# Hybrid decoder step on one core: the samples' latent scores from three matmuls, high and low queries side by side

## What is computed

```python
def _mla_sample(q_nope, q_rope, ckv, kr, cache_ckv, cache_kr, page_table, w_uk, w_uv):
    past_c = cache_ckv[page_table].reshape(DB, -1, MLA_KV_RANK)      # 2048 positions x 128
    past_r = cache_kr[page_table].reshape(DB, -1, MLA_ROPE)          # 2048 positions x 32
    c_all = jnp.concatenate([past_c, ckv], axis=1)
    r_all = jnp.concatenate([past_r, kr], axis=1)
    q_lat = jnp.einsum("bthd,chd->bthc", q_nope, w_uk.reshape(MLA_KV_RANK, H, MLA_NOPE))
    s = (jnp.einsum("bthc,bsc->bhts", q_lat, c_all)
         + jnp.einsum("bthr,bsr->bhts", q_rope, r_all)).astype(jnp.float32) * MLA_SCALE
    mask = jnp.arange(P + T)[None, :] <= (P + jnp.arange(T))[:, None]
    p = jax.nn.softmax(jnp.where(mask, s, NEG), axis=-1)
    o_lat = jnp.einsum("bhts,bsc->bthc", p.astype(c_all.dtype), c_all)
```

## Time and profile before

| | us |
|---|---|
| three runs | 1795.09, 1804.6, 1806.44 |
| median | 1804.6 |
| span of the profiled execution | 1796.1 |
| TensorE busy | 1722.8 (96%) |
| TensorE weight loads busy | 1506.7 (84%) |
| VectorE busy | 858.5 (48%) |
| ScalarE busy | 661.3 (37%) |
| GpSimd busy | 578.2 (32%) |

### The profile page before, as it was taken

One profiled execution on the slowest core, in us unless ns is written; L12 is line 12 of the kernel. 1 busy time (PEld: TensorE's weight loads), 2 busy tenths in 40 slices (PEclk: granted clock), 3 DMA queues, 4 the chain that ended last, 5 costly groups with the idle time before them and its releaser, 6 DMA issues.

```text
span 1796.1 us, 27967 instructions
## 1 busy us (share of the span) xinstructions
PE 1722.8 (96%) x9949; PEld 1506.7 (84%) x9949; DVE 858.5 (48%) x1800; ACT 661.3 (37%) x1326; POOL 578.2 (32%) x535
## 2 busy tenths in 40 slices
PE   7999989999997999999999999999999999999996
PEld 6788878888886888888788989888898898888985
DVE  6433336667675776766443332433423333334235
ACT  5222125667675666565422312212112121121113
POOL 1000004566561877668301312212113122121221
PEclk9999987999999999999999999999999999999999
DMA  8232243323207565655612668486595775956812
GB/s 281 103 105 94 95 124 104 93 58 101 77 7 180 166 187 154 168 159 166 219 47 52 136 137 141 124 166 112 116 156 128 154 122 125 166 110 134 150 46 104
DMA packets 156061, 227.44 MB, mean 127 GB/s; under 512 B 31063, under 2 KB 128984, under 8 KB 149528
## 3 DMA queue, kind: packets, MB, share of 16 engines
q1 hardware_dynamic: 153086, 159.39, 30.0%
q0 software_dynamic: 2880, 66.85, 22.4%
HBM read 201.12 MB, written 91.93 MB: 163 GB/s over the span
## 4 chain that ended last, share of the span: by engine, by line
PE 48%; DMA 2%; ACT 1%; DVE 1%; POOL 0%; issue 0%; SPq 0%; ACTq 0%; DVEq 0%; POOLq 0%
PE wide L2582 22%; PE turn L2604 14%; PE rest L2583 7%; PE wide L2266 4%; DMA out_y_prompt<-f_gc 1%; PE wide L2681 1%; DMA o_work<-scratch_s_o 0%; DMA acc<-in_w_gate 0%; PE turn L2278 0%; DVE f_gc L2560 0%; ACT f_gc L2497 0%; PE rest L2589 0%; POOL f_gl L2660 0%; ACT f_rows L2504 0%; POOL f_st L2428 0%
## 5 line engine op out<-in xcount | busy, mean ns | idle before, releaser
L2604 PE MATMUL turn<-lead,f_ah 128*128 128x512 f32 x792 | 245.6, 391 | 4.7 <-DVE f_al L2548 4.0
L2517 DVE TENSOR_TENSOR acc<-turn,acc 128x512 f32<-128x512 f32 x198 | 136.6, 691 | 197.5 <-PE turn L2604 197.5
L2582 PE MATMUL wide<-hT_h,lead 128*128 128x512 f32 x704 | 184.9, 354 | 0.0
L2604 PEld LDWEIGHTS turn<-lead,f_ah 128*128 128x128 f32 x792 | 148.2, 189 | 36.5 <-DVE f_al L2548 4.2
L2385 POOL TENSOR_TENSOR f_gl<-f_graw,f_gh 128x1024 fp32r<-128x1024 f32 x21 | 50.6, 2408 | 351.6 <-ACT f_gh L2435 351.6
L1054 POOL TENSOR_SCALAR a_pr<-a_pr,a_rden 128x256 f32<-128x256 f32 (+7 forms) x128 | 94.3, 747 | 191.6 <-DVE a_rden L1154 187.0
L2604 PE MATMUL turn<-lead,f_al 128*128 128x512 f32 x396 | 154.8, 391 | 0.0
L2531 DVE SCALAR_TENSOR_TENSOR f_gc<-wide,f_coef,f_gc 128x832 f32<-128x832 f32 x44 | 47.7, 1085 | 209.6 <-ACT f_lasts L2455 206.7
L761 PE MATMUL zp<-win_h,xT_h 128*128 128x512 f32 (+1 forms) x288 | 113.0, 392 | 3.3 <-DVE acc L632 3.3
L761 PE MATMUL zp<-win_l,xT_h 128*128 128x512 f32 (+1 forms) x288 | 111.7, 388 | 0.0
L761 PE MATMUL zp<-win_h,xT_l 128*128 128x512 f32 (+1 forms) x288 | 111.7, 388 | 0.0
(11 more groups left out here) (362 smaller groups left out, 4437.3 us busy)
## 6 DMA issues: line engine op xcount, KB each, us to landing
out_s_win_k<-in_state_win_k POOLq DMA_DIRECT2D x10, 3264.0 KB, 41.8
out_s_win_v<-in_state_win_v POOLq DMA_DIRECT2D x10, 3264.0 KB, 44.4
acc<-in_state_win_k SPq DMA_DIRECT2D x16, 768.0 KB, 6.1
acc<-in_state_win_v SPq DMA_DIRECT2D x16, 768.0 KB, 5.6
f_uraw<-in_w_up SPq DMA_DIRECT2D x22, 512.0 KB, 4.4
f_draw<-in_w_down SPq DMA_DIRECT2D x11, 1024.0 KB, 33.0
f_graw<-in_w_gate SPq DMA_DIRECT2D x21, 512.0 KB, 7.9
acc<-in_cache_kv_latent SPq DMA_DIRECT2D x128, 64.0 KB, 1.8
```

The lines of the kernel that those rows point to most:

```text
L2517: nc.vector.tensor_tensor(a, dp[h][:], a, ALU.add).then_inc(S["d_add"], 1)
L2582: nc.tensor.matmul(out[:, c0:c1], w[n][:, k, :], x[:, k, c0:c1], start=s, stop=e)
L2604: last = nc.tensor.matmul(dp[h][:], a[:, c, t * P:(t + 1) * P], w[:, c, h * 512:(h + 1) * 512], start=(c == 0 and j == 0), stop=(c == 1 an ...
```

## The change

The queries' high and low parts now lie in one tile m_qhl, in the order high of sample 0, low of sample 0, high of sample 1, and so on, with a strip of 64 zero columns at the end, which GpSimd clears at the block's start (semaphore q_pad; ScalarE waits for it ahead of the cast m_qr). 128 neighbouring columns are then the high and the low queries of one sample. With them as weights, a product with the high keys gives rows 0 to 63 of the bank the high queries' part and rows 64 to 127 the low queries'. A product with the low keys follows with the same weights, and the rotary product with 64 weight columns goes to rows 0 to 63: three matmuls of 512 columns. `bank_use` of event s becomes "hd": ScalarE copies rows 64 to 127 into half of the tile a_own (this tile is used by the second attention block alone before), and VectorE's instruction adds that copy where it added zeros. The copy adds a low-queries-by-low-keys term that was not there before. Event s_new keeps four matmuls, with the rotary one at another place, and its result lies in rows 0 to 63.

```diff
-        self.q_h, self.q_l = sb("m_qh", [P, DEC_B, NS], F32R), sb("m_ql", [P, DEC_B, NS], F32R)
+        self.q_hl = sb("m_qhl", [P, 2 * DEC_B + 1, NS], F32R)
+        self.q_h, self.q_l = (self.q_hl[:, 0:2 * DEC_B, :].rearrange("p (b x) n -> p b x n", x=2)[:, :, x, :] for x in range(2))
         self.q_r = sb("m_qr", [3 * ROPE, DEC_B, NS], F32R)
+        self.s_low = [prompt.own[i * NS:(i + 1) * NS] for i in range(2)]
...
-        if e[0] in ("s", "s_new"):
+        if e[0] == "s_new":
             return "d"
-        if e[0] in ("pre_uk", "pre_qn", "pre_new", "pre_lat", "cT", "fold", "p", "p_new"):
+        if e[0] in ("pre_uk", "pre_qn", "pre_new", "pre_lat", "cT", "s", "fold", "p", "p_new"):
             return "hd"
...
     def gpsimd(self, pool, e):
         S, nc = self.S, self.nc
+        if e[0] == "setup":
+            nc.gpsimd.memset(self.q_hl[:, 2 * DEC_B, :].bitcast(F32), 0.0).then_inc(S["q_pad"], 1)
...
         elif k == "pre_qr":
+            act.wait_ge(S["q_pad"], 1)
...
+        elif k == "s":
+            g = e[1]
+            if g >= 2:
+                self.ring.done(act, ("s", g - 2))
+            nc.scalar.copy(self.s_low[g % 2], bank[NS:P]).then_inc(R["bank_hi"], 1)
...
         elif k in ("s", "s_new"):
             b, h = divmod(e[1], 4) if k == "s" else (e[1], 4)
             rows = self.half(b)
-            bank = self.ring.ready(dve, e)
             if k == "s":
-                src, tab, cols = bank[rows, :], self.zero[rows, 0:512], slice(512 * h, 512 * h + 512)
+                bank = self.ring.hi(dve, e)
+                src, tab, cols = bank[0:NS, :], self.s_low[e[1] % 2], slice(512 * h, 512 * h + 512)
             else:
-                src, tab, cols = bank[rows, 0:DEC_T], self.fresh[rows, :], slice(PAST, PAST + DEC_T)
+                bank = self.ring.ready(dve, e)
+                src, tab, cols = bank[0:NS, 0:DEC_T], self.fresh[0:NS, :], slice(PAST, PAST + DEC_T)
             if e == ("s_new", 0):
                 dve.wait_ge(S["const"], 64)
-                dve.wait_ge(self.zero_in, 16)
...
-                last = nc.tensor.matmul(out, a, b, start=(i == 0), stop=(i == len(terms) - 1))
+                last = nc.tensor.matmul(out[0:a.shape[1]], a, b, start=(i == 0), stop=(i == len(terms) - 1))
...
-            pair = slice(b - b % 2, b - b % 2 + 2)
-            flat = lambda t: t[:, pair, :].rearrange("p a n -> p (a n)")
-            qh, ql, qr = flat(self.q_h), flat(self.q_l), flat(self.q_r)
+            flat = lambda n: self.q_hl[:, n:n + 2, :].rearrange("p a n -> p (a n)")
+            qh, ql, qr = flat(2 * b), flat(2 * b + 1), self.q_r[:, b, :]
...
-                product(out, ((qh, x), (qh, xl), (ql, x), (qr, y))).then_inc(R["bank_ps"], 1)
+                product(out, ((qh, x), (qr, y), (qh, xl))).then_inc(R["bank_ps"], 1)
...
-                product(out, ((qh, x), (qh, xl), (ql, x), (qr, y))).then_inc(R["bank_ps"], 1)
+                product(out, ((qh, x), (qr, y), (qh, xl), (ql, x))).then_inc(R["bank_ps"], 1)
```

More of the change, by code:

```diff
@@ L1272, in __init__ @@
             "const q_in w_in new_in c_new0 c_new1 c_new2 qn_ok q3_h q3_l w_h w_l rw3_h rw3_l pre_h "
-            "r3_h r3_l c_hi cs neg_go turn_go exp recip stored").split()}
+            "r3_h r3_l c_hi cs neg_go turn_go exp recip stored q_pad").split()}
         for i in range(3):
@@ L1475, in mine @@
     def mine(self, t, i):
-        return t[:].rearrange("p b (i e t) -> p e b i t", i=PAIRS, e=2)[:, i]
+        return t.rearrange("p b (i e t) -> p e b i t", i=PAIRS, e=2)[:, i]
     def latent(self, bank):
```

## The result

| | median us | lowest to highest | ratio to before, 95% interval |
|---|---|---|---|
| before, 20 runs beside it | 1799.22 | 1793.18 to 1806.44 | |
| after, 20 runs (the range leaves out one of 3382.04) | 1806.69 | 1800.58 to 1809.75 | 1.0038 (1.0028 to 1.0049) |

What follows compares the result with a forecast made beforehand. TensorE, busy in 96% of the span, was taken to set the pace. Removed matmuls of -7.4 us plus 2.5 us of added waits gave -4.9 us, from the median 1804.6 to 1799.7, forecast as 1800; range 1788 to 1810.

Steps and rivals of the forecast that it cites:

- the likeliest case: Whole kernel: 3 to 7 us below the median, given 45%; the forecast itself was a gain of 4.9 us.
- 32 x 0.23 = 7.4 us removed: TensorE, first attention block: one of four matmuls goes from each of 32 score products, at a pitch of 0.23 us.
- Copies in ScalarE's idle time: ScalarE, first attention block: 32 copies of 0.58 us, 18.6 us in all, mostly land in idle time before m_rt casts.
- The delay of VectorE, 16 starts and 7.4 us: VectorE's score instruction waits for the copy: 16 starts move by more than 0.1 us, some 7.4 us in sum.
- The laying: All 32 copies placed on the trace of before, each behind its preceding ScalarE instruction, to estimate VectorE's later starts.
- I take the 4.7 us of VectorE waits growing by half, 2.5 us: TensorE's waits on VectorE in the block: added cost taken as 2.5 us, between bounds of nothing and 18.6.
- Nothing arrives: Rival, 22%: TensorE reaches its next wait earlier for the same late result; waits grow by 7.4 us, giving 1804.6.
- ScalarE's queue: Rival, 12%: prompt exponentials behind the copy must wait for the product; the kernel becomes slower, 1810.4.
- the 5.8 us term: Exponentials queued behind ScalarE's copy at four places start 1.2 to 1.6 us late each, some 5.8 us in sum.
- The clock rival: Rival, 6%: more TensorE waits bring five more low-clock stretches of 1.7 us, 8.5 us in all, giving 1808.2.
- The full gain: Rival, 15%: nothing of the removed matmuls' time is given back, -7.4 us, giving 1797.2.
- What would show it: Signs in the block's rows: TensorE's waits on VectorE about 7 us, block ending about 5 us earlier; three conditions for being wrong.

Runs made afterwards that it cites:

- e3: Kernel before, plus 32 ScalarE copies at the same queue places, waiting for the product but reading a zero table, with nobody waiting for them: 1799.35 us, ratio 1.0008.
- e2: Kernel before with its four matmuls, plus 32 unused ScalarE copies of 512 columns that VectorE waits for: 1807.76 us, ratio 1.0061.
- e1: Changed kernel without ScalarE's copies; VectorE adds zeros and waits for TensorE alone, low queries' part left out: 1795.11 us, ratio 0.9987.
- k2: Three matmuls and the copy only at the 19 groups where VectorE came before a copy could be ready, otherwise as the kernel before: 1804.37 us, ratio 1.0033.
- k4: The kernel before, unchanged, run again for a second profile: 1800.06 us, ratio 1.0011.
- f2: Changed kernel with VectorE's instruction on the scores six places later and ScalarE's copy three places later: 1818.61 us, ratio 1.0130.
- f3: Changed kernel with the 32 copies made by VectorE right ahead of its own instruction, none on ScalarE: 1823.79 us, ratio 1.0146.
- e4: The changed kernel, unaltered, run again for a second profile: 1803.85 us, ratio 1.0034.
- f4: Kernel before with four matmuls, plus 32 unused ScalarE copies of only 8 columns that VectorE waits for: 1801.76 us, ratio 1.0025.

## Why the prediction was wrong

The time was forecast at 1800 and came out at 1806.69, inside the range of 1788 to 1810 and inside the 1% band. The direction of the likeliest case was wrong, and that the number lies so near is in part luck: 1800 was counted from 1804.6, the median of three runs, and the 20 runs of before beside the change have 1799.22. The same gain of 4.9 us from there would be 1794.3. By its steps:

- **32 x 0.23 = 7.4 us removed: right.** The rest of the block's account falls from 229.6 to 222.9, 6.7 us; over all runs by about 7. The pitch of three is the same, 0.23 us: 341.04, 341.27, 341.51.

```profile
341.04 0.39 PE L1567 MATMUL a_bank<-m_cth,m_qhl 128*128 128x512 f32 x1
341.27 0.40 PE L1567 MATMUL a_bank<-m_rt,m_qr 96*64 96x512 f32 x1
341.51 0.39 PE L1567 MATMUL a_bank<-m_ctl,m_qhl 128*128 128x512 f32 x1
```

- **Copies in ScalarE's idle time: right.** 582 ns, x32, and e3 shows that this work and its place cost nothing that can be told. ScalarE's idle time before m_rt fell from 17.9 to 7.5 us, as said.
- **The delay of VectorE, 16 starts and 7.4 us: too small.** In e2, with the four matmuls of before, 20 starts lie more than 0.1 us later behind their product and the sum is 11.4 us; from e1 to after it is 12.1. The laying let VectorE start when the copy ends (332.10 becomes 332.6), while the traces have 0.21 us between the two; over 19 groups that is up to 4.0 us. And "elsewhere VectorE arrived late by itself and the copy is ready by then" is wrong for ten groups: besides the nine of the earlier trace rows, VectorE came at ten more before a copy could be ready.
- **"I take the 4.7 us of VectorE waits growing by half, 2.5 us": this step failed.** TensorE's waits on VectorE went from 4.8 (in the whole block) to 11.9 us (10.3 of them in the groups shown), all its waits from 7.8 to 14.4. Two parts make this up. The copies bring 4.6 us (e1's 9.8 to 14.4) of the 12.1 us of delay, and in e2 3.1 of 11.4; the share taken, a third, was near, and the delay was what was small. (With the clock, the copies cost 8.9 us of block on three matmuls and 6.9 on four.) The other 2.0 come without any copy (7.8 to 9.8 in e1): TensorE with fewer matmuls reaches the same late results sooner. The sum put that at nothing. What stands behind the scores on VectorE (m_ctl, a_kl, a_pl) is exactly what TensorE waits for in the earlier trace rows, and at 393 us nearly all of the delay arrived, 0.87 of 0.92. k2 shows that the cost sits at the groups where VectorE would have started before a copy is ready.
- **The clock, put at nothing in the sum: this failed too.** Of the 11.8 us between the 6.7 us gained and the 5.1 lost, waits are 6.6 and the lower clock 5.2 (10.3 us more of it, at half). Without this term the block would have ended within 0.1 us of before. I had it as a rival of its own with 6%. Its size is the least sure of the terms: against k4's profile of the same kernel before, the block is 4.0 us longer, the waits 6.8 and the lower clock only some 7 us more, 3.4 at half. That the added waits draw it is argued from where it falls, behind them, and not shown: waits and low clock don't go in proportion (f2 has 25.2 us of waits and 13.7 of low clock, f3 22.6 and 34.1). Why the one draws more than the other stays open. The sum as measured in the block: -6.7 + 6.6 + 5.2 = +5.1.
- **The rivals.** Nothing arrives: the waits grew by 6.6, near its 7.4, but it left out the clock. ScalarE's queue: e3 has the queue blocked in the same way and shows no loss (its interval ends 4.5 us above before), so the 5.8 us term isn't there; its time of 1810.4 was near for another reason. The clock rival asked for five more stretches of 1.7 us; 10.3 us more low clock make 5.2 us, three of them. The full gain isn't reached even without the copy: e1 keeps 3.8 us of 7 in the block, since TensorE comes earlier to the same late results (waits +2.0, low clock +3.4, which k4 has too).
- **What would show it**: of the conditions named for being wrong, the new stretch at the lower clock came true, at 400 us. The other, TensorE's waits more than doubled, is met only just: over the 296 to 530 us of the earlier trace rows they go from 6.1 to 12.8 us, over the whole block from 7.8 to 14.4. The third, transposes of a_pr that wait for GpSimd, isn't among TensorE's waits. The block ended 3.9 us later instead of 5 earlier.

Between the loss of 5.1 us in the block and the 8.3 us between the two profiled spans, 4.4 us arose after the block and 1.1 were gained ahead of it. In e4, the same kernel as after, only 1.2 us arose after the block. The work there is the same, and what differs is the time at the lower clock behind the block: 25.9 us in before, 35.4 in after, 28.8 in e4, and 32.7 in k4, where 3.0 us arose with no change at all. Half of each difference is about the time that arose. Which executions draw it stays open.

## What to carry to other kernels

An engine with idle time can take a copy for nothing, but the engine that then waits for the copy pays for it. Count the delay at every place where the waiting engine would have started before the copy is ready, from the copy's end and the step behind it; here three to four tenths of that sum came out as waits of TensorE, at one place nearly all. Beside the waits expect time at the lower clock, here half to four fifths of their growth, by which profile of before it is counted. A removed matmul in front of a late result is worth half to two thirds of its time here (e1: 3.8 of 7 us against before, 4.9 against k4), and 7 us of saved work don't pay for one more engine in the chain, 32 times over.

## What of the hardware was not expected

- **The step through one more engine costs the copy's own length and hardly more.** At 331.45 and 342.52 us the copies end, and VectorE starts at 331.66 and 342.73, 0.21 us later each time:

```profile
330.87 0.58 ACT L1450 COPY a_own<-a_bank 64x512 f32<-64x512 f32 x1
331.66 0.75 DVE L1538 CUSTOM_DVE_ANT_0 m_p<-a_bank,a_own,m_st 64x512 f32<-64x512 f32 x1 [2.68 <-ACT a_own L1450]
```

  That is not an added price, though: before, VectorE started 0.22 us after the end of TensorE's last matmul (331.88 to 332.10). Where the copy finds ScalarE free, VectorE starts 0.83 us after the product's end for 0.22, with the copy of 8 columns 0.41 (338.88 to 339.29 in f4): 0.61 and 0.19 us later, with copies of 0.58 and 0.16. Matmul ends are modelled, so the last hundredths are not to be read. What comes on top is the place in the queue: where the copy stands behind a cast, even the tiny one is later (0.74 us after the product at 391 us).

  The Trainium skill ("Perfetto Trace Analysis", Per-instruction lifecycle) says why a profile shows such a gap: the recorded end of an instruction of VectorE or ScalarE comes before its semaphore update has reached the other engines. No run here shows what the 0.21 us is made of.
- **The clock fell behind waits of 1 to 2 us.** Ahead of 350 us TensorE waited 1.09 us at 347.00 and 1.58 at 349.84 (before: 0.28 and 1.51). Over 350 to 354 us the granted clock is then 0.50, the level of 1.2 GHz, and over 350 to 362 us it is 0.61 against 0.86. Not every such wait is followed by it: in e2 TensorE waited 2.02 us at 401.39, and over 399 to 410 us the granted clock is 1.00. The lines of after:

```profile
347.00 0.44 PE L1203 MATMUL a_bank<-a_kh,a_qh 96*128 96x384 f32 x1 [1.09 <-DVE m_ctl L1493]
...
349.84 0.55 PE L1228 MATMUL a_o<-a_ph,a_vh 128*128 128x256 f32 x1 [1.58 <-DVE a_pl L1158]
...
350.00:354.00 4.00, 4.00 (x13) 3.13 (x13) 1.59 (x8) 1.40 (x5) 1.15 (x2) 0.50 0.56 164
```

  The Trainium skill ("TensorE: Matmul & The Clock Gate", The HAM clock gate) says that the clock knows two levels only and that idleness brings the lower one. The 0.50 agrees with the level. Stretches of full use, too, run at the lower level: TensorE was busy in all 12 us from 350 to 362.
